# Two stacks in one launch: a pooled projection tile moved between the two compression products of the attention layers

## The reference

```
proj = h @ w_in[l]                      # 1024 -> 22 tiles of up to 128 columns
nsa:  kc, vc = gelu(windows(k or v) @ w1) @ w2     # the compression, 32 taps of 64x64
      scores over compressed keys, over selected blocks and over a window
gla:  gated linear attention in chunks of 64
pool: y = (window mean of u - u) @ w_pool   # u = two tiles of proj ("pooled branch")
h = layer_norm(alpha*h + concat(nsa, gla, pool) @ w_out)
h = layer_norm(alpha*h + relu(h @ w_up)^2 @ w_down)
```

## Time and profile before

| | |
|---|---|
| median of 3 runs | 1461.5 us (1461.16 to 1461.75) |
| the profiled execution, its own time | 1462.19 us |
| its span in the profile | 1460.4 us |
| PE busy | 1399.4 us, 96% of the span |
| DVE, ACT, POOL busy | 1053.6, 832.3 and 518.2 us |
| mean granted TensorE clock | 0.987 |
| share of PE in the chain that ended last | 76% |
| share of DVE and ACT in it | 13% and 7% |

### The profile page before, as it was taken

How to read it: one execution, slowest core, us unless ns; L and a number is a source line. 1 busy time by engine, 2 the same in 40 slices (tenths; PEclk the granted TensorE clock), 3 DMA queues, 4 the chain that set the end, 5 groups by cost and what they waited for, 6 DMA issues and landing times.

```text
span 1460.4 us, 29915 instructions
## 1 busy us (share of the span) xinstructions
PE 1399.4 (96%) x12819; PEld 1178.7 (81%) x12819; DVE 1053.6 (72%) x1361; ACT 832.3 (57%) x1253; POOL 518.2 (35%) x420
## 2 busy tenths in 40 slices
PE   5999999999999999999999999999899999999997
PEld 3878888887778888878678788887777778788886
DVE  3888986557797885558686888766767774898853
ACT  4566544336674544446885656544576767576651
POOL 0123896112145991225210465401212112146620
PEclk9989999999989999999999999999999999999999
DMA  8443466554333665534336365553434233556550
GB/s 332 170 145 116 145 213 210 187 190 149 115 115 116 229 205 202 198 103 163 115 114 233 117 202 187 174 194 107 151 113 141 76 114 116 202 179 205 192 177 29
DMA packets 35700, 235.21 MB, mean 161 GB/s; under 512 B 4720, under 2 KB 6768, under 8 KB 8816
## 3 DMA queue, kind: packets, MB, share of 16 engines
q1 hardware_dynamic: 35568, 233.31, 46.7%
HBM read 232.24 MB, written 1.05 MB: 160 GB/s over the span
## 4 chain that ended last, share of the span: by engine, by line
PE 76%; DVE 13%; ACT 7%; issue 2%; DMA 1%; SPq 1%; DVEq 0%; ACTq 0%
PE psum L689 23%; PE psum L690 23%; PE psum L691 23%; DVE low L2102 4%; PE psum L777 2%; DVE arena L2492 2%; ACT high L1500 2%; DMA raw<-stream 1%; ACT m L1850 1%; DVE m L2560 1%; PE psum L1009 1%; DVE arena L2563 1%; PE psum L992 1%; ACT arena L1987 0%; ACT L1984 0%
## 5 line engine op out<-in xcount | busy, mean ns | idle before, releaser
L2102 DVE SCALAR_TENSOR_TENSOR low<-raw,high 128x2048 f16<-128x2048 f32 (+4 forms) x246 | 525.8, 2143 | 259.5 <-ACT high L1500 259.3
L689 PE MATMUL psum<-u,high 128*128 128x256 f16 (+4 forms) x2168 | 599.8, 277 | 26.7 <-DVE low L2102 15.4
L690 PE MATMUL psum<-u,high 128*128 128x256 f16 (+4 forms) x2168 | 598.9, 276 | 0.0
L691 PE MATMUL psum<-u,low 128*128 128x256 f16 (+4 forms) x2168 | 598.9, 276 | 0.0
L1500 ACT ACTIVATE high<-raw 128x2048 f16<-128x2048 f32 (+4 forms) x246 | 419.1, 1709 | 136.5 <-PE psum L691 126.3
L689 PE MATMUL psum<-arena,high 128*128 128x256 f16 (+2 forms) x1264 | 346.7, 274 | 2.8 <-ACT arena L1835 1.5
L690 PE MATMUL psum<-arena,high 128*128 128x256 f16 (+2 forms) x1264 | 346.6, 274 | 0.0
L691 PE MATMUL psum<-arena,low 128*128 128x256 f16 (+2 forms) x1264 | 346.6, 274 | 0.0
L689 PEld LDWEIGHTS psum<-u,high 128*128 128x128 f16 (+2 forms) x2168 | 213.0, 98 | 71.6 <-issue 21.7
L690 PEld LDWEIGHTS psum<-u,high 128*128 128x128 f16 (+2 forms) x2168 | 213.3, 98 | 31.6 <-issue 0.7
L691 PEld LDWEIGHTS psum<-u,low 128*128 128x128 f16 (+2 forms) x2168 | 213.3, 98 | 31.2
(11 more groups left out here) (324 smaller groups left out, 1468.6 us busy)
## 6 DMA issues: line engine op xcount, KB each, us to landing
raw<-stream SPq DMA_DIRECT2D x208, 1024.0 KB, 4.9
raw<-stream SPq DMA_DIRECT2D x8, 768.0 KB, 4.1
con<-consts SPq DMA_DIRECT2D x1, 1758.0 KB, 12.4
raw<-stream SPq DMA_DIRECT2D x3, 512.0 KB, 3.6
raw<-stream SPq DMA_DIRECT2D x2, 712.0 KB, 5.6
h<-x_t SPq DMA_DIRECT2D x1, 1024.0 KB, 5.7
out_t<-h SPq DMA_DIRECT2D x4, 256.0 KB, 2.4
raw<-stream SPq DMA_DIRECT2D x1, 896.0 KB, 5.5
```

Source lines behind the costliest of these rows:

```text
L689: pe.matmul(out, w_hi, x[0], start=start, stop=False)
L690: pe.matmul(out, w_hi, x[1], start=False, stop=False)
L691: return pe.matmul(out, w_lo, x[0], start=False, stop=stop)
L2102: tell(dve.scalar_tensor_tensor(low[:, at:at + w], raw[:, off:off + w], W_SCALE, high[:, at:at + w], ALU.mult, ALU.subtract), split_ready ...
```

## The change

In each of the two layers TensorE runs `one(T_PU + 1)` directly behind `compressed_hidden(0)`, and no longer behind `turn(2)`. ScalarE's copy of this tile (`evac(T_PU + 1)`) moves from behind `copy_pt(2)` to behind `give(8)`. The orders of VectorE, GpSimd and SP stay.

```diff
@@ first_layer of the tensor engine
                 turn(0)
                 compressed_hidden(0)
+                one(T_PU + 1)
                 scores(2)
                 values(0)
                 turn(1)
...
                 scores(3)
                 values(1)
                 turn(2)
-                one(T_PU + 1)
                 compressed_keys()
                 scores(4)
@@ first_layer of the scalar engine
                 exps(1)
                 copy_pt(0)
                 give(8)
+                evac(T_PU + 1)
                 exps(2)
                 copy_pt(1)
                 copy_out(0)
...
                 exps(3)
                 copy_out(1)
                 copy_pt(2)
-                evac(T_PU + 1)
                 act.wait_ge(kcvc_done, l + 1)
```

## The result

The changed kernel takes 1480.05 us (median of 6 runs, 1472.82 to 1485.7) beside 1462.08 us for the kernel before in the same session (6 runs, 1461.16 to 1464.27). The ratio is 1.0122, with a 95% interval of 1.0097 to 1.0147: slower by 18 us. The forecast was 1478.7 us, 17.2 us slower.

The account below looks back on a forecast made before the run. TensorE was taken to bound most of the span, VectorE and ScalarE the stretch up to `turn(2)`. Delay 4.1 plus clock 4.6 made 8.7 us in the second layer, 8.5 in the first: 17.2 us, so 1478.7 us, range 1465 to 1486.

Parts of the forecast that it names:

- The sign: Whole kernel: slower with chance 0.87, same 0.10, faster 0.03.
- The wait: Ahead of `scores(2)`: the moved tile waits 1.9 us for the weights that `give(7)` converts until 396.00.
- The tile: Ahead of `scores(2)`: 24 matmuls begin at half clock and lift it, 3.9 us, bounds 2.62 and 5.1.
- GpSimd beside VectorE: Pooled chain beside VectorE's pace-setting links: small VectorE operations lose 1.1 us in all, bounds 0 and 2.0.
- The start of `scores(4)`: On TensorE behind `exps(3)`, second layer: 415.5, so 4.1 us late, bounds 1.7 and 6.2.
- The clock behind it: From `scores(4)` through `turn(3)` half clock costs 3.7 us, part of `T_OG` 0.9: together 4.6, bounds 0 and 6.6.
- the rival in which the clock comes back while `scores(4)` and what follows run: Behind `scores(4)`: clock kept or soon back, only the delay costs; 1469.5 us, between 1465 and 1474; chance 0.23.
- The rivals with no loss: Tile fills TensorE's gap ahead of `scores(2)` without waiting: 1460 to 1462 us, chance 0.10; or faster, 1459.9 us, chance 0.03.

Follow-up runs that it names:

- dummy_new: Kernel before, tile at its old place, plus 24 dummy matmuls ahead of `scores(2)` behind the wait for the weights of `give(7)`: 1470.67 us, ratio 1.0053.
- copy_late: Changed kernel with ScalarE's copy of the tile back at its old place behind `copy_pt(2)`: 1477.54 us, ratio 1.0107.
- awake: Changed kernel plus 24 dummy matmuls behind `turn(2)`, where the tile stood before: 1474.59 us, ratio 1.0084.
- wait_only: Kernel before with only the moved tile's wait for its weights added ahead of `scores(2)`, tile at its old place: 1462.56 us, ratio 1.0002.
- first profile: Profiled execution of the changed kernel in its first session, beside the kernel before: 1485.7 us.
- second profile: Changed kernel run again unaltered in another session: profiled execution 1474.52 us, median 1476.62 us, ratio 1.0117 to the kernel before.
- give7_tile: Changed kernel with `give(7)` on VectorE moved from ahead of `weigh(1)` to between `maxima(0)` and `weigh(0)`: 1479.43 us, ratio 1.0113.
- all_undone: Changed kernel with `give(7)` early, ScalarE's copy at its old place, and 12 dummy matmuls on each side of `turn(2)`: 1474.69 us, ratio 1.0078.
- dense_mid: Kernel before plus 16 dummy matmuls behind `turn(1)`, ahead of the second compression product: 1461.75 us, ratio 1.0001.
- give7_alone: Kernel before with only `give(7)` moved early on VectorE, between `maxima(0)` and `weigh(0)`: 1461.00 us, ratio 0.9992.
- give7_dense: Kernel before with `give(7)` early in both layers and 16 dummy matmuls behind `turn(1)`: 1461.06 us, ratio 0.9991.
- mixed: Kernel before with 16 dummy matmuls behind `turn(1)` in both layers and `give(7)` early in the second layer only: 1460.37 us, ratio 0.9986.

## Why the prediction was right

The sign was right, and so was the chain of causes: the wait and the tile ahead of `scores(2)`, GpSimd beside VectorE, the half clock behind `scores(4)`. dummy_new, copy_late and awake show the three parts one by one. The sizes of the terms were less good than the total, and that the total came within 1.4 us of the median is in part luck: 1478.7 us lies in the gap between the two groups of times (1477.5 and 1483.9), where none of the twelve runs fell.

*The wait* was forecast at 1.9 us and measured at 1.95. That it costs nothing by itself was in the numbers (`weigh(1)` ends at 397.0) but not said; wait_only shows it. What delays `maxima(2)` is the wait and the tile's length together.

*The tile* was forecast at 3.9 us with bounds of 2.6 and 5.1. It took 4.2 us in the second layer of the first profile, and 5.1 in the first. The near hit in the second layer is luck. I had the clock fall ahead of the tile and the tile bring it back; in fact the tile began at full clock, the clock fell at 408.8 with the tile under way and came back at 412.2, behind its end at 411.9. In the first layer all of the tile ran at half clock (84.5 to 91.3), so in neither did it run faster by lifting the clock. `maxima(2)` was 3.7 us late by the forecast and 4.3 and 5.3 by the profile.

*GpSimd beside VectorE* was sized at 1.1 us and cost 1.6. Two openings and not three took part: the two small operations. The first long conversion took 2.38 us in one profile and 2.51 in the other beside 2.28 before, and the second 2.29 as before; two of GpSimd's operations beside them took 2.97 and 3.14 us instead of 1.04.

*The start of `scores(4)`* was forecast 4.1 us late. It was 5.4 us late in the second layer and 6.3 in the first. That is the sum of the two terms above less 0.5 and 0.7 us, which the missing tile gave back; the forecast took 0.7 and 0.9.

*The clock behind it* was forecast at 4.6 us a layer. It cost 5.3 us where the clock stayed low into `T_OG`, and 1.5 to 1.6 us where it came back earlier. Here one reading was wrong. I wrote that scores, values and transposes do not bring the clock back alone, and that `T_OG` does. In the second profile of the changed kernel it came back at 427.2 during the compressed scores, with no dense tile before it. So the rival in which the clock comes back while `scores(4)` and what follows run holds for this clock term in a part of the executions (seven of the twelve, if the two groups of times are the two lengths that the two profiles show), though not for the time that I gave it (1469.5 us), since the delay was larger than I took. The Trainium skill, TensorE: Matmul & The Clock Gate, Part 1, "What's actually happening", says that sustained work brings the full rate back; one profile agrees, and the other, busy from 428.33 on without a gap, was at 0.50 until 439.5.

The delay was sized 1.3 us too small in the second layer and 2.4 in the first, where the forecast had 3.9. The clock was 0.7 us too small in one profile and 3 us too large in the other. So between `scores(1)` and `scores(5)` the two layers together lost 22.2 us in the first profile and 13.9 in the second, where the forecast had 17.2. The median of the first six runs lies between the groups, which is why the total fits better than the terms. In the second session the median was 1476.62 us, still in the range.

*The rivals with no loss* assumed no wait for the weights. In the second layer of give7_tile the wait was gone and `maxima(2)` was 0.6 us late, nearly as that rival has it, and yet `scores(5)` was 7.2 us late, 5.4 of it by the clock. So its own condition would not have saved it. That a dense tile behind `turn(2)` would have is argued from awake and dummy_new; all_undone, which was to show it, did not.

## What to carry to other kernels

Before moving dense matmuls out of a place, look what they do to the clock there: for a tile that stands directly ahead of the part where TensorE sets the pace this was worth 5.3 us a layer in one profile and 1.5 to 1.6 in the other, beside its own 2.6 us. In the part where other engines set the pace half clock cost little: dense_mid shortened it and won 0.5 and 0.7 us. Before moving work into a gap, compare the gap (0.34 us) with the work (2.6 us at best), and see when its inputs are ready and who is queued behind it. And when a producer moves, follow its other consumers: here an earlier copy put GpSimd's chain beside VectorE's critical small operations, for 1.6 us a layer.

## What the runs showed of the hardware

TensorE's clock can stay at half while the engine is busy without a gap. In the changed kernel it was at 0.50 from 428.33 until 439.5: up to 435.8 with float32 scores, values, small products and transposes, and then for 3.7 us with the dense float16 matmuls of `T_OG`. In all_undone it was at 0.50 from 418.2 to 424.9, of which all but the last 0.8 us was such float32 work. In the changed kernel's other profile the clock came back at 427.2, inside the float32 work that `scores(4)` had begun at 423.66. It differs from execution to execution, with `maxima(2)` and `scores(4)` in the second layer alike within 0.1 us, and the two profiled executions are 11 us apart. I did not find out what decides it.

TensorE can stand still with no semaphore behind it, for 0.5 to 2.4 us. Where a trace has such a stall it lies inside one of the two compression products or, once, in the moved tile. The kernel before has one too, of 1.46 us, in the second compression product of the first layer. What the seven stalls around the place have in common is a 16 KB packet of the instruction queue q8, which the trace shows moving shortly before with a load of 270 to 300 GB/s ahead of it: TensorE goes on 1.24 to 1.46 us after the end of that packet each time (before, wait_only, give7_tile, give7_alone, give7_dense, and twice in all_undone). In give7_alone the packet moved from 83.45 to 84.38, behind the load that an earlier conversion had let start. In the kernel before and in mixed, where that load is not yet moving, it moved from 80.97 and 80.89, and TensorE had no stall there. Such a packet can also pass without a stall (in the kernel before from 400.28 to 401.24). So the traces fit instructions that came late behind a weight load. No experiment moved the instruction packet alone, and whose instructions it carries is not shown.
